# First norm of a hybrid encoder: mean squares for two token tiles at a time, and a later copy of the first weight tile's high half

## The chip, the cores and the metric

The kernel runs on one core of a Trainium2 chip. The metric is the device time of one execution in microseconds; lower is better. A core has five engines that work side by side, each through its own queue of instructions in order: TensorE (PE, with weight loads as PEld), VectorE (DVE), ScalarE (ACT), GpSimd (POOL) and SyncE (SP), which here issues the transfers. They wait for each other by semaphores.

## The reference

One encoder layer on 1024 + 512 tokens of width 1024, in float32. The change is in the first norm and the start of the projection that follows it:

```
u = x * rsqrt(mean(x * x) + 1e-6) * norm1
p = u @ W_in            # W_in: 1024 x 7696, for three mixers and their gates
x = x + W_out(sum_b sigmoid(G_b(u)) * (o_b @ W_br[b]))
x = x + relu(RMSNorm(x) @ W1)^2 @ W2
y = RMSNorm(x)
```

The three mixers are neighbourhood attention, a gated delta rule and a gated linear recurrence.

## The kernel before

Every large product is made of three float32r matmuls (`mm3`, L102 to L104): both factors are split into a high half, which is a rounded copy, and a low half, which is the rest. ScalarE makes the high halves, GpSimd the low ones.

The function `front` holds the first norm and the projection. The 1536 tokens are 12 tiles of 128. For each token tile j:

- ScalarE squares the tile and sums each row (`square`, L518), into column j of `ss`.
- VectorE makes mean + epsilon and its reciprocal for a group of G = 4 tiles at once (`mean`, L672 and L674), ScalarE the square root into `rstd` (L540).
- VectorE scales the tile by `rstd` into `xn`, which has two buffers (L695).
- TensorE transposes it in two halves of four 128 x 128 blocks into `turn` (`turn_half`, L612), in PSUM.
- VectorE multiplies by the norm's gain into `uf` (`gain_tile`, L686, two halves); this reads PSUM.
- ScalarE copies the high half into `u_hi` (L545), GpSimd subtracts to get `u_lo` (L488).

The weights come in column tiles of 128 (`load_w`), with `high_w` on ScalarE (L512) and `low_w` on GpSimd (L482), two buffers. TensorE first transposes tiles 0 to 3. Then it projects weight tiles 0 and 1 on three token blocks of 512 tokens, each behind `ul_done` of its four token tiles; within the first two blocks, one `turn_half` of the tiles 4 to 11 is put behind every second k step, that is behind every six matmuls. After that, weight tiles 2 to 60 are projected on all tokens. SyncE loads weight tile 2 only after `zeroed`, which GpSimd gives behind its last `u_lo`.

The queues are written out by hand. ScalarE's order at the start is: squares 0 to 3, high half of weight tile 0, then for each group its root, and for each tile in it the square of the tile four further on and the copy to `u_hi`; the high half of weight tile 1 follows tile 3. GpSimd's order is: low half of weight tile 0, `u_lo` of tiles 0 to 3, low half of weight tile 1, `u_lo` of tiles 4 to 11. VectorE's order within a group is `xn` of tile j, then the gain of tile j - 1; at the first tile of a group it is the gain of tile j - 1, the mean, then `xn` of tile j:

```
for j in range(NT):
    if j and j % G == 0:
        gain_tile(j - 1)
    if j % G == 0:
        mean(j)
    ...
    dve.tensor_scalar(xn[:, j % 2], x[:, j % XR], rstd[:, j:j + 1], None, ALU.mult).then_inc(normed, 1)
    if j % G:
        gain_tile(j - 1)
```

Of the kernel before, what the change touches and what calls it, by code (L numbers as in the profile page):

```python
# [17 lines left out]
ACT = mybir.ActivationFunctionType  # L18
ALU = mybir.AluOpType
# [3 lines left out]
D = 1024  # L23
# [3 lines left out]
NT = T // P  # L27
TB = 512
NTB = T // TB
EPS = 1e-6  # L30
# [206 lines left out]
def front(nc, sources, gain, w, proj, o_t, conv_w, conv_b, w_r, b_r, w_i, b_i, lam, u_hi, u_lo, ident, ones, rpb, v_mid, near,  # L237
# [6 lines left out]

    CT = BW // P
    G = 4
    XR = 8
    tiles = []
    for i in range(CT):
# [24 lines left out]
    with Space(nc, "pj") as s:  # L274
# [3 lines left out]
        with ExitStack() as early:  # L278
            def sb(name, shape):
                return early.enter_context(nc.sbuf_tensor(f"pj_{name}", [P] + shape, F32))  # L280
            x, xn, uf, junk = sb("x", [XR, D]), sb("xn", [2, D]), sb("uf", [2, KD, P]), sb("junk", [D])
        xpad, xc, gt = s.sb("xpad", [PADW]), s.sb("xc", [T]), s.sb("gt", [T])
# [14 lines left out]
        ss, ms, rr, rstd = (s.sb(v, [NT]) for v in ("ss", "ms", "rr", "rstd"))  # L297
# [43 lines left out]
        def _(sp):  # L341
            def load_x(t):
                if t >= XR:
                    sp.wait_ge(normed, t - XR + 1)
                sp.dma_start(x[:, t % XR], sources[t]).then_inc(x_in[t], 16)

            def load_w(n):
                if n >= 2:
                    sp.wait_ge(lo_done, n - 1)
                c = column(tiles[n])  # L350
                sp.dma_start(w_raw[:, n % 2], w_t[:, :, c:c + P]).then_inc(w_in[n % 2], 16)
# [49 lines left out]
            def bias_tables(p):  # L401
# [18 lines left out]
                if 26 <= p < 26 + NR:  # L420
# [5 lines left out]
                                 near[:, :, o * NA_COLS:o * NA_COLS + KEYS]).then_inc(bias_set, 16)  # L426
            for t in range(G):
                load_x(t)
                if t == 1:
                    sp.dma_start(gcol[:], gain.rearrange("(k p) -> p k", p=P), allow_slow_non_contiguous=True).then_inc(gained, 16)  # L430
            load_w(0)
            for t in range(G, NT):
                load_x(t)
                if t == G + 1:
                    load_w(1)
# [43 lines left out]
        def _(pool):  # L479
            def low_w(n):  # L480
                pool.wait_ge(hi_done, n + 1)
                pool.tensor_tensor(w_lo[:, n % 2], w_raw[:, n % 2], w_hi[:, n % 2].bitcast(F32), ALU.subtract).then_inc(lo_done, 1)  # L482
# [3 lines left out]
            for j in range(NT):  # L486
                pool.wait_ge(uh_done, j + 1)
                pool.tensor_tensor(u_lo[:, :, j * P:(j + 1) * P], uf[:, j % 2],  # L488
                                   u_hi[:, :, j * P:(j + 1) * P].bitcast(F32), ALU.subtract).then_inc(ul_done, 1)
                if j == G - 1:  # L490
                    low_w(1)
# [15 lines left out]
        def _(act):  # L507
            def high_w(n):
                act.wait_ge(w_in[n % 2], n // 2 * 16 + 16)
                if n >= 2:  # L510
                    act.wait_ge(mm_done, n - 1)
                act.copy(w_hi[:, n % 2], w_raw[:, n % 2]).then_inc(hi_done, 1)  # L512

            def square(j):
                act.wait_ge(x_in[j], 16)
                if j:
                    act.wait_ge(squared, j)
                act.activation(junk[:], x[:, j % XR], ACT.Square, accum_out=ss[:, j:j + 1]).then_inc(squared, 1)  # L518

# [6 lines left out]
            def decay(i, d):  # L526
# [5 lines left out]
                act.activation(rt[:], a[:], ACT.Square).then_inc(a2_done, 1)  # L532
                act.wait_ge(v_done, 2 * i + d + 1)
                act.activation(rt[:], rt[:], ACT.Sqrt).then_inc(rt_done, 1)
            for j in range(G):
                square(j)
            high_w(0)
            for j0 in range(0, NT, G):
                act.wait_ge(recip, j0 // G + 1)
                act.activation(rstd[:, j0:j0 + G], rr[:, j0:j0 + G], ACT.Sqrt).then_inc(rooted, 1)  # L540
                for j in range(j0, j0 + G):
                    if j + G < NT:
                        square(j + G)
                    act.wait_ge(scaled, 2 * j + 2)
                    act.copy(u_hi[:, :, j * P:(j + 1) * P], uf[:, j % 2]).then_inc(uh_done, 1)  # L545
                    if j == G - 1:
                        high_w(1)
# [120 lines left out]
        @block.vector  # L668
        def _(dve):
            def mean(j0):  # L670
                dve.wait_ge(squared, j0 + G)
                dve.tensor_scalar(ms[:, j0:j0 + G], ss[:, j0:j0 + G], 1.0 / D, EPS, ALU.mult, ALU.add).then_inc(rstd_in, 1)  # L672
                dve.wait_ge(rstd_in, j0 // G + 1)
                dve.reciprocal(rr[:, j0:j0 + G], ms[:, j0:j0 + G]).then_inc(recip, 1)  # L674
                dve.wait_ge(rooted, j0 // G + 1)

            def gain_tile(j):
                if j == 0:
                    dve.wait_ge(gained, 16)
                if j >= 2:  # L680
                    dve.wait_ge(uh_done, j - 1)
                    dve.wait_ge(ul_done, j - 1)
                for half in range(2):
                    k = slice(half * (KD // 2), (half + 1) * (KD // 2))
                    dve.wait_ge(turned, 2 * j + half + 1)
                    dve.tensor_tensor(uf[:, j % 2, k], turn[:, half], gcol[:, k].unsqueeze(2).to_broadcast([P, KD // 2, P]),  # L686
                                      ALU.mult).then_inc(scaled, 1)
            for j in range(NT):
                if j and j % G == 0:
                    gain_tile(j - 1)  # L690
                if j % G == 0:
                    mean(j)
                if j >= 2:
                    dve.wait_ge(turned, 2 * (j - 1))
                dve.tensor_scalar(xn[:, j % 2], x[:, j % XR], rstd[:, j:j + 1], None, ALU.mult).then_inc(normed, 1)  # L695
                if j % G:
                    gain_tile(j - 1)
            gain_tile(NT - 1)

# [400 lines left out]
def deltanet(nc, proj, g_rows, cols, masks, o_t, conv_w, norm_w, ident, ones):  # L1100
# [10 lines left out]
    with Space(nc, "dn") as s:  # L1111
# [151 lines left out]
        def _(act):  # L1263
# [29 lines left out]
            def main(i, more):  # L1293
# [23 lines left out]
                for k in range(NS):  # L1317
                    act.wait_ge(S["s_mm"], i * NS + k + 1)
                    if k == 0:
                        act.wait_ge(S["amat"], i * 12 + 12)  # L1320
                    if k >= 4:
                        act.wait_ge(S["u_mm"], i * VT + 6 + k - 3)
                    act.copy(sbuf_s[k % 4], ps[:, k % 2]).then_inc(S["s_ev"], 1)
                    if T_LAG <= k < NTR + T_LAG:
                        turned(k - T_LAG)
                    u = k + 2 * NTB
                    if i and u == OUT_AT["squares"]:
                        out_squares(i - 1)
                    if i and u == OUT_AT["root"]:
                        out_root(i - 1)  # L1330
                    if more:
                        front(i + 1, u)
                    if u == ZTANH_AT:
                        act.wait_ge(S["z_in"], i * 16 + 16)
                        act.activation(th[:, 1], zt, ACT.Tanh, scale=0.5).then_inc(S["zt"], 1)
# [14 lines left out]
            for u in range(UNITS):  # L1350
                front(0, u)
# [5 lines left out]
        def _(pe):  # L1357
# [29 lines left out]
            def main(i, more):  # L1387
# [40 lines left out]
                for step in range(NS + T_LAG):  # L1428
# [12 lines left out]
                    if U_LAG <= step < NS + U_LAG:  # L1441
                        k = step - U_LAG
                        n = k % 6
                        pe.wait_ge(S["s_ev"], i * NS + k + 1)

                        pe.wait_ge(S["u_ev"], i * VT + 6 + k - 1)
                        for j in range(4):
                            last = pe.matmul(ps[:, 5 + 2 * (k % 2), j], sbuf_s[k % 4][:, j], un[:, n, j], start=True, stop=True)
                        last.then_inc(S["u_mm"], 1)
                        if i and 6 + k == OUT_AT["lengths"]:  # L1450
                            out_lengths(i - 1)
                        if i and 6 + k in OUT_AT["spread"]:
                            out_spread(i - 1, OUT_AT["spread"].index(6 + k), 3)
                        if more:
                            front(i + 1, 6 + k)
# [883 lines left out]
```

## Time and profile before

| | |
|---|---|
| median of 3 runs | 3469.65 us (3467.18 to 3469.73) |
| the profiled execution | 3468.34 us, span 3466.6 us |
| TensorE matmuls busy | 3187.0 us, 92% of the span |
| VectorE, ScalarE, GpSimd busy | 1314.3, 1073.4, 1180.3 us |
| mean granted TensorE clock | 0.951 |

In the rows below, a row of the timeline gives the start in us from the span's start, the duration in us, the engine, the line and operation, what is written <- what is read, and how many instructions are merged (x). A bracket gives the idle time of the engine ahead of it and what ended that. A merged row's duration runs from the first start to the last end. A tile is named without its buffer, so the token tiles are told by their order.

### The profile page before, as it was taken

Reading aid. Unit: us, or ns where it says so; the run is one execution under the profiler, and the core shown is the slowest. Engines: PE = TensorE matmul, PEld = TensorE weight load, DVE = VectorE, ACT = ScalarE, POOL = GpSimd, SP = SyncE. Lnnn points to the kernel's source line nnn. Section 1 sums busy time; section 2 is a strip of 40 time slices with the busy share of each in tenths; the row PEclk is TensorE's granted clock in tenths of the full one; section 3 lists DMA queues with packets and bytes.
Section 4 is the critical chain, followed back from the end, with each engine's and each line's share of the span. In section 5 each row is a group of like instructions: output and inputs, shape, how many; then the busy total and the mean of one; then the engine's idle time right before and its main releaser. Section 6 shows DMA issues by size and latency. Waiting matters only on the chain. (4 is left out here: it accounts for less than half of the span.)

```text
span 3466.6 us, 40721 instructions
## 1 busy us (share of the span) xinstructions
PE 3187.0 (92%) x16275; PEld 2654.2 (77%) x16275; DVE 1314.3 (38%) x1975; ACT 1073.4 (31%) x1691; POOL 1180.3 (34%) x761
## 2 busy tenths in 40 slices
PE   6999999999998957969696979998999999999998
PEld 4888888888886636869595958786888888888887
DVE  4232323111001877575766433511222323232323
ACT  3222222321112734434343421223233333323222
POOL 4111111111113021121212014244666566666664
PEclk9999999999999977979797989998999999999999
DMA  3433233433323620001000045443332232333331
GB/s 110 164 131 107 77 110 99 128 100 118 130 79 143 201 95 28 19 28 37 28 19 1 19 143 170 140 143 118 98 98 97 85 98 97 122 98 97 97 122 61
DMA packets 235946, 334.04 MB, mean 96 GB/s; under 512 B 32368, under 2 KB 185712, under 8 KB 235760
## 3 DMA queue, kind: packets, MB, share of 16 engines
q1 hardware_dynamic: 235760, 331.44, 29.2%
q8 instruction: 131, 2.15, 0.2%
q14 instruction: 55, 0.45, 0.0%
HBM read 254.27 MB, written 86.93 MB: 98 GB/s over the span
## 5 line engine op out<-in xcount | busy, mean ns | idle before, releaser
L102 PE MATMUL pj_acc<-u_hi,pj_w_hi 128*128 128x512 f32 x1464 | 582.9, 398 | 14.7 <-POOL u_lo L488 13.0
L104 PE MATMUL pj_acc<-u_hi,pj_w_lo 128*128 128x512 f32 x1464 | 571.8, 391 | 0.0
L103 PE MATMUL pj_acc<-u_lo,pj_w_hi 128*128 128x512 f32 x1464 | 571.4, 390 | 0.0
L2256 DVE TENSOR_TENSOR x_tm<-m_ps,x_tm 128x512 f32<-128x512 f32 x384 | 265.0, 691 | 745.0 <-PE m_ps L104 745.0
L482 POOL TENSOR_TENSOR pj_w_lo<-pj_w_raw,pj_w_hi 128x1024 fp32r<-128x1024 f32 x61 | 148.0, 2427 | 826.3 <-ACT pj_w_hi L512 826.3
L102 PEld LDWEIGHTS pj_acc<-u_hi,pj_w_hi 128*128 128x128 f32 x1464 | 275.9, 188 | 77.8 <-POOL u_lo L488 13.9
L2133 POOL TENSOR_TENSOR m_w_lo<-m_w_raw,m_w_hi 128x1024 fp32r<-128x1024 f32 x96 | 237.6, 2498 | 263.2 <-ACT m_w_hi L2047 263.2
L103 PEld LDWEIGHTS pj_acc<-u_lo,pj_w_hi 128*128 128x128 f32 x1464 | 276.0, 189 | 61.8 <-issue 5.7
L104 PEld LDWEIGHTS pj_acc<-u_hi,pj_w_lo 128*128 128x128 f32 x1464 | 275.7, 188 | 57.8
L102 PE MATMUL m_ps<-m_v_hi,m_w_hi 128*128 128x512 f32 x768 | 299.9, 390 | 2.4 <-DVE m_v_lo L2224 2.4
L103 PE MATMUL m_ps<-m_v_lo,m_w_hi 128*128 128x512 f32 x768 | 299.7, 390 | 0.0
L104 PE MATMUL m_ps<-m_v_hi,m_w_lo 128*128 128x512 f32 x768 | 299.7, 390 | 0.0
L102 PE MATMUL m_ps<-m_w_hi,m_h_hi 128*128 128x512 f32 x768 | 299.6, 390 | 0.0
L104 PE MATMUL m_ps<-m_w_hi,m_h_lo 128*128 128x512 f32 x768 | 298.9, 389 | 0.0
L103 PE MATMUL m_ps<-m_w_lo,m_h_hi 128*128 128x512 f32 x768 | 298.8, 389 | 0.0
L2126 POOL TENSOR_TENSOR m_w_lo<-m_w_raw,m_w_hi 128x1024 fp32r<-128x1024 f32 x96 | 227.9, 2396 | 23.0 <-ACT m_w_hi L2040 23.0
L1865 POOL TENSOR_TENSOR mo_w_lo<-mo_w_raw,mo_w_hi 128x512 fp32r<-128x512 f32 x72 | 94.1, 1307 | 357.0 <-ACT mo_w_hi L1832 357.0
L512 ACT CAST pj_w_hi<-pj_w_raw 128x1024 fp32r<-128x1024 f32 x61 | 63.9, 1047 | 404.5 <-PE pj_acc L104 392.2
L2047 ACT CAST m_w_hi<-m_w_raw 128x1024 fp32r<-128x1024 f32 x96 | 96.0, 1049 | 247.8 <-PE m_ps L104 247.8
L102 PEld LDWEIGHTS m_ps<-m_v_hi,m_w_hi 128*128 128x128 f32 x768 | 144.8, 189 | 33.0 <-DVE m_v_lo L2224 2.8
L2059 ACT CAST m_h_hi<-m_rel 128x512 fp32r<-128x512 f32 x96 | 59.7, 622 | 356.4 <-POOL m_rel L2139 356.4
L104 PEld LDWEIGHTS m_ps<-m_v_hi,m_w_lo 128*128 128x128 f32 x768 | 144.7, 188 | 30.2
(258 smaller groups left out, 5605.4 us busy)
## 6 DMA issues: line engine op xcount, KB each, us to landing
m_w_raw<-in_w_mlp_dram SPq DMA_DIRECT2D x48, 1024.0 KB, 5.4
m_w_raw<-in_w_mlp_dram SPq DMA_DIRECT2D x96, 512.0 KB, 3.3
proj<-pj_stage SPq DMA_DIRECT2D x61, 768.0 KB, 3.4
pj_w_raw<-in_w_in_dram SPq DMA_DIRECT2D x61, 512.0 KB, 4.7
mo_gate<-proj SPq DMA_DIRECT2D x24, 768.0 KB, 4.2
mo_w_raw<-in_w_out_dram SPq DMA_DIRECT2D x48, 256.0 KB, 2.8
rpb_bias<-pj_shut SPq DMA_DIRECT2D x48, 192.0 KB, 3.0
rpb_bias<-rpb_near SPq DMA_DIRECT2D x24, 384.0 KB
```

The lines of the kernel that those rows point to most:

```text
L102: pe.matmul(out, w_hi, x_hi, start=first, stop=False)
L103: pe.matmul(out, w_hi, x_lo, start=False, stop=False)
L104: return pe.matmul(out, w_lo, x_hi, start=False, stop=last)
L482: pool.tensor_tensor(w_lo[:, n % 2], w_raw[:, n % 2], w_hi[:, n % 2].bitcast(F32), ALU.subtract).then_inc(lo_done, 1)
L512: act.copy(w_hi[:, n % 2], w_raw[:, n % 2]).then_inc(hi_done, 1)
L1865: pool.tensor_tensor(w_lo[:, sl % 2], w_raw[:, sl % 3], w_hi[:, sl % 2].bitcast(F32), ALU.subtract).then_inc(w_lo_done, 1)
L2047: act.copy(w2_hi[:, (2 * gg + j) % 4], w2_raw[:, j]).then_inc(w2_hi_done, 1)
L2059: act.copy(h_hi[:, m % 4], rel[:, j]).then_inc(hh_done, 1)
L2126: pool.tensor_tensor(w1_lo[:, m % 4], w1_raw[:, :, j * P:(j + 1) * P], w1_hi[:, m % 4].bitcast(F32), ALU.subtract).then_inc(w1_lo_done, 1)
L2133: pool.tensor_tensor(w2_lo[:, m % 4], w2_raw[:, j], w2_hi[:, m % 4].bitcast(F32), ALU.subtract).then_inc(w2_lo_done, 1)
L2256: dve.tensor_tensor(xt, ps2[:, q % 4], xt, ALU.add).then_inc(added, 1)
```

## The change

A second group size GS = 2 takes the place of G in ScalarE's and VectorE's queues: the mean, the reciprocal and the root are made for two tiles at a time, six times in place of three; ScalarE squares two tiles ahead in place of four. `high_w(0)` is moved from behind the first four squares to behind square 3, which now comes after the copy of tile 0 and ahead of the copy of tile 1. `high_w(1)`, the orders of TensorE, GpSimd and SyncE, and all shapes of large tiles stay as they are.

```diff
     G = 4
+    GS = 2
 ...
-            for j in range(G):
+            for j in range(GS):
                 square(j)
-            high_w(0)
-            for j0 in range(0, NT, G):
-                act.wait_ge(recip, j0 // G + 1)
-                act.activation(rstd[:, j0:j0 + G], rr[:, j0:j0 + G], ACT.Sqrt).then_inc(rooted, 1)
-                for j in range(j0, j0 + G):
-                    if j + G < NT:
-                        square(j + G)
+            for j0 in range(0, NT, GS):
+                act.wait_ge(recip, j0 // GS + 1)
+                act.activation(rstd[:, j0:j0 + GS], rr[:, j0:j0 + GS], ACT.Sqrt).then_inc(rooted, 1)
+                for j in range(j0, j0 + GS):
+                    if j + GS < NT:
+                        square(j + GS)
+                    if j == 1:
+                        high_w(0)
                     act.wait_ge(scaled, 2 * j + 2)
                     act.copy(u_hi[:, :, j * P:(j + 1) * P], uf[:, j % 2]).then_inc(uh_done, 1)
 ...
             def mean(j0):
-                dve.wait_ge(squared, j0 + G)
-                dve.tensor_scalar(ms[:, j0:j0 + G], ss[:, j0:j0 + G], 1.0 / D, EPS, ALU.mult, ALU.add).then_inc(rstd_in, 1)
+                dve.wait_ge(squared, j0 + GS)
+                dve.tensor_scalar(ms[:, j0:j0 + GS], ss[:, j0:j0 + GS], 1.0 / D, EPS, ALU.mult, ALU.add).then_inc(rstd_in, 1)
 ...
             for j in range(NT):
-                if j and j % G == 0:
+                if j and j % GS == 0:
                     gain_tile(j - 1)
-                if j % G == 0:
+                if j % GS == 0:
                     mean(j)
 ...
-                if j % G:
+                if j % GS:
                     gain_tile(j - 1)
```

## Rows read from the trace of the kernel before

**Rows 1.** Windows: busy time and count of each engine, then clock and DMA.

```profile
88.00:1100.00 1012.00, 1004.78 (x4344) 814.84 (x4342) 222.40 (x166) 209.84 (x192) 168.09 (x70) 1.00 0.34 109
```

**Rows 2.** Waits of TensorE from 0 to 90 us: total, times, longest.

```profile
PE pj_acc L102 <- POOL u_lo L488: 13.0, 3, 4.5
```

**Rows 3.** Timeline of ScalarE, 8 to 21 us.

```profile
8.55 0.19 ACT L518 ACTIVATION_READ_ACCUMULATOR pj_junk<-pj_x 128x1 f32 x1
...
13.06 1.04 ACT L512 CAST pj_w_hi<-pj_w_raw 128x1024 fp32r<-128x1024 f32 x1 [0.60 <-DMA pj_w_raw<-in_w_in_dram]
14.12 1.28 ACT L540 ACT_TABLE_LOAD   x1
15.41 0.20 ACT L540 ACTIVATE pj_rstd<-pj_rr 128x4 f32<-128x4 f32 x1
...
19.87 1.05 ACT L545 CAST u_hi<-pj_uf 128x1024 fp32r<-128x1024 f32 x1 [3.21 <-DVE pj_uf L686]
20.82 1.06 ACT L518 ACTIVATE pj_junk<-pj_x 128x1024 f32<-128x1024 f32 x1
```

**Rows 4.** Timeline of ScalarE around a later table load.

```profile
167.75 1.28 ACT L534 ACT_TABLE_LOAD   x1
169.64 1.49 ACT L534 ACTIVATE pj_rt<-pj_rt 128x1536 f32<-128x1536 f32 x1 [0.60 <-DVE pj_rt L721]
```

**Rows 5.** Timeline of VectorE, 15 to 18 us.

```profile
15.65 1.43 DVE L695 TENSOR_SCALAR pj_xn<-pj_x,pj_rstd 128x1024 f32<-128x1024 f32 x1 [2.78 <-ACT pj_rstd L540]
...
17.01 0.74 DVE L695 TENSOR_SCALAR pj_xn<-pj_x,pj_rstd 128x1024 f32<-128x1024 f32 x1
```

**Rows 6.** Timeline of GpSimd, 14 to 34 us.

```profile
14.19 2.35 POOL L482 TENSOR_TENSOR pj_w_lo<-pj_w_raw,pj_w_hi 128x1024 fp32r<-128x1024 f32 x1 [10.24 <-ACT pj_w_hi L512]
20.99 10.03 POOL L488 TENSOR_TENSOR u_lo<-pj_uf,u_hi 128x1024 fp32r<-128x1024 f32 x4 [4.46 <-ACT u_hi L545]
30.97 2.82 POOL L482 TENSOR_TENSOR pj_w_lo<-pj_w_raw,pj_w_hi 128x1024 fp32r<-128x1024 f32 x1
```

**Rows 7.** Timeline of three engines, group border ahead of tile 8.

```profile
47.65 0.69 DVE L686 TENSOR_TENSOR pj_uf<-pj_turn,pj_gcol 128x512 f32<-128x512 f32 x1 [1.04 <-PE pj_turn L612]
48.26 0.16 DVE L672 TENSOR_SCALAR pj_ms<-pj_ss 128x4 f32<-128x4 f32 x1
48.38 1.04 ACT L545 CAST u_hi<-pj_uf 128x1024 fp32r<-128x1024 f32 x1 [1.55 <-DVE pj_uf L686]
...
49.33 0.20 ACT L540 ACTIVATE pj_rstd<-pj_rr 128x4 f32<-128x4 f32 x1
49.50 2.34 POOL L488 TENSOR_TENSOR u_lo<-pj_uf,u_hi 128x1024 fp32r<-128x1024 f32 x1 [1.26 <-ACT u_hi L545]
...
49.56 2.83 DVE L695 TENSOR_SCALAR pj_xn<-pj_x,pj_rstd 128x1024 f32<-128x1024 f32 x1 [0.93 <-ACT pj_rstd L540]
```

**Rows 8.** Timeline of VectorE: second half of tile 5's gain.

```profile
40.35 0.69 DVE L686 TENSOR_TENSOR pj_uf<-pj_turn,pj_gcol 128x512 f32<-128x512 f32 x1 [1.04 <-PE pj_turn L612]
```

**Rows 9.** Timeline of TensorE: restarts and transposes of the first two blocks.

```profile
31.08 0.80 PE L102 MATMUL pj_acc<-u_hi,pj_w_hi 128*128 128x512 f32 x1 [4.48 <-POOL u_lo L488]
...
36.07 0.60 PE L612 MATMUL pj_turn<-ident,pj_xn 128*128 128x128 f32 x4
...
41.54 0.60 PE L612 MATMUL pj_turn<-ident,pj_xn 128*128 128x128 f32 x4
...
51.89 0.79 PE L102 MATMUL pj_acc<-u_hi,pj_w_hi 128*128 128x512 f32 x1 [4.28 <-POOL u_lo L488]
...
56.73 0.60 PE L612 MATMUL pj_turn<-ident,pj_xn 128*128 128x128 f32 x4
```

**Rows 10.** Windows, the restart of the second block.

```profile
51.80:54.60 2.80, 2.71 (x6) 2.04 (x7) 1.25 (x2) 0.00 (x0) 0.04 (x1) 0.50 0.00 0
```

**Rows 11.** Timeline of TensorE: first matmuls after two shorter waits.

```profile
86.88 0.50 PE L102 MATMUL pj_acc<-u_hi,pj_w_hi 128*128 128x512 f32 x1 [1.68 <-POOL pj_w_lo L482]
...
2250.36 0.80 PE L102 MATMUL mo_ps<-mo_w_hi,mo_held 128*128 128x512 f32 x1 [2.77 <-POOL mo_w_lo L1865]
```

More of the change, by code:

```diff
@@ L670, in mean @@
             def mean(j0):
-                dve.wait_ge(squared, j0 + G)
-                dve.tensor_scalar(ms[:, j0:j0 + G], ss[:, j0:j0 + G], 1.0 / D, EPS, ALU.mult, ALU.add).then_inc(rstd_in, 1)
-                dve.wait_ge(rstd_in, j0 // G + 1)
-                dve.reciprocal(rr[:, j0:j0 + G], ms[:, j0:j0 + G]).then_inc(recip, 1)
-                dve.wait_ge(rooted, j0 // G + 1)
+                dve.wait_ge(squared, j0 + GS)
+                dve.tensor_scalar(ms[:, j0:j0 + GS], ss[:, j0:j0 + GS], 1.0 / D, EPS, ALU.mult, ALU.add).then_inc(rstd_in, 1)
+                dve.wait_ge(rstd_in, j0 // GS + 1)
+                dve.reciprocal(rr[:, j0:j0 + GS], ms[:, j0:j0 + GS]).then_inc(recip, 1)
+                dve.wait_ge(rooted, j0 // GS + 1)
             def gain_tile(j):
```

## The prediction

> **What bounds the kernel now.** I read the page's waits of TensorE first, then the opening 90 us instruction by instruction on each engine, since every edit lies in the first norm. After that opening the front stage is all TensorE: it is busy 1004.78 of the 1012 us from 88 to 1100 [rows 1], so nothing behind can swallow time lost or won in front. In the opening, TensorE waits 13.0 us in three places for GpSimd's `u_lo` [rows 2]: before the first, second and third token block of the projection. The three waits are alike: TensorE turns the last tile of the next block, then VectorE's gain, ScalarE's `u_hi`, GpSimd's `u_lo` follow one another and TensorE starts. So the opening is one chain: start of the first block, then eight steps of six matmuls and four transposes, the wait, eight more steps, the wait. Weights two and on are loaded behind `zeroed`, which GpSimd gives after its last `u_lo`; they move with the chain. The time changes by what `u_lo` of tile 11 moves by.
>
> **Removed at the start.** ScalarE's first root stands behind four squares, the weight's high half and a table load; it starts at 15.41 [rows 3]. After the change it stands behind two squares. The second square's sum ends at 8.55 + 0.19 = 8.74. The table load of 1.28 us is put ahead of a single wait: elsewhere it ran from 167.75 and the square root it serves came 0.60 us after it ended, waiting for VectorE [rows 4]. So the load runs at once, hides the mean (0.16 us [rows 7]) and a reciprocal of like size, and the root starts at 10.03: 5.4 us earlier. That is all that could ever be won.
>
> **What is left of it.** From root to `u_hi` of tile 0 was 4.46 us, of which 1.43 - 0.74 = 0.69 is VectorE's first `xn` lying in wait while GpSimd's low half of the weight ran until 16.54 [rows 5, 6]. GpSimd is idle at 10 us, so `u_hi` starts at 10.03 + 3.77 = 13.80. But the weight's high half now stands behind the copy of tile 0 and square 3: 0.95 us for the copy (the next instruction starts at 20.82 behind 19.87) and 1.06 for the square with the short read of its sum partly under it put it at 15.83, and it ends at 16.87. GpSimd's queue has the low half in front of every `u_lo`: it runs from 16.96 to 19.31 (2.35 [rows 6]), and `u_lo` of tile 0 can start at 19.31 against 20.99. So only 1.7 of the 5.4 us are left: the copy was moved past, and took GpSimd's queue with it. The four `u_lo` took 10.03 us in a row. In them one instruction was stretched by a waiting `xn`; now a second `xn` (tile 2, whose root comes after the moved copy) waits for the low half and gets in ahead of the next one. Such a stretch costs 2.82 against 2.35, 0.47 us [rows 6]. The first block starts 1.7 - 0.5 = 1.2 us earlier. Bounds: 1.7 without the stretch, 0 if ScalarE's order delays tile 1 more than I see.
>
> **Added at tile 6 and tile 10.** With four in a group, `xn` of the next tile is issued ahead of the gain of the one before, except at tile 4 (in front of the first block, where it is hidden by GpSimd) and tile 8. At tile 8 the trace shows the price of a border [rows 7]: gain second half at 47.65, mean at 48.26, root at 49.33 because it stands behind the copy of tile 7 at 48.38, and `xn` at 49.56, where GpSimd's `u_lo` had started at 49.50. `xn` took 2.83 in place of 0.74: it came free only after the 2.34 us of `u_lo`. That is 49.56 + 2.83 - 47.65 = 4.74 us from gain to `xn`. At tile 8 it costs nothing: TensorE is waiting for the block anyway, and the next transposes come six matmuls later.
>
> Groups of two put the same border at tiles 6 and 10, in the midst of the eight steps, where TensorE's queue has the transposes between matmuls. Gain of tile 5 starts at 40.35 [rows 8]; plus 4.74 is 45.09, and the transposes of tile 6, which ran at 41.54 [rows 9], start at about 45.15: TensorE stands for 3.6 us. All matmuls of the first block stand behind them in order, then tile 7's transposes, and so `u_lo` of tile 7, which the second block waits for. None of it is hidden. Tile 10 repeats the pattern with the same steps in the second block: 3.6 again. The three small instructions of an extra border are in these 4.74 us; the squares that its mean needs stand in ScalarE's queue ahead of the copy of tile 5 and are ready. The extra border at tile 2 lies in front of the first block: its root waits for the copy of tile 1, and its `xn` then waits for the low half, which is the term of the start's sum above.
>
> What makes `xn` wait is weighed here against the skill. The row shows an `xn` of 2.83 us under a running `u_lo`, 0.74 otherwise, while the gain, which reads PSUM, keeps its 0.69 at all times. The Trainium skill, SBUF — State Buffer, section "Who interferes with whom", says that a two-port VectorE instruction and a GpSimd instruction take one port pair by lock for the whole instruction, whoever issues first. By that rule the trace agrees: `u_lo` led by 0.06 us at tile 8. By a lost lead the sum would be that of the second rival.
>
> **The clock.** At the blocks' starts TensorE comes back from 4.28 and 4.48 us of idleness at a granted clock of 0.50, 1.2 GHz [rows 10]. Restart to the second group of transposes took 56.73 - 51.89 = 4.84 and 36.07 - 31.08 = 4.99 us [rows 9]. At full clock three steps took 41.54 - 36.07 = 5.47, 1.82 each; the same stretch is two steps less one group of transposes (0.60 or under), 3.04 to 3.64. So a slow restart costs 1.2 to 1.9 us; I take 1.6. Does a stall of 3.6 us make the clock fall? After 2.77 us idle the first matmul took 0.80, as at half clock; after 1.68 it took 0.50 [rows 11]. 3.6 lies above the gap that was followed by a fall, so I take the fall at both: 3.2 us. The Trainium skill, TensorE: Matmul & The Clock Gate, section "What's actually happening", says that the slow state is the default, that activity releases it, and that the watch on activity does not start anew with a kernel. The trace agrees in that a gap of 2.77 us was enough; by this rule the two stalls could fare differently, which is the case of one escape below.
>
> **Sum.** -1.2 + 2 x 3.6 + 2 x 1.6 = +9.2 us. The profiled execution lasted 3468.34 (span 3466.6), so 3477.5; against the median of the runs, 3469.65, which is 1.3 above it, 3478.9. The rest of the kernel is unchanged.
>
> **Rivals.**
> - *The clock holds* through both stalls: +6.0, 3475.7. For it: the time of a fall follows something I can't place, and a gap of 1.68 left the clock alone. Against: the 2.77 us gap. If one stall of two escapes: +7.6, 3477.3.
> - *`xn` takes the port first.* At the border `xn` and `u_lo` are 0.06 us apart [rows 7]. If `xn` comes first it takes 0.74, gain to `xn` is 2.65, and each stall is 40.35 + 2.65 + 0.06 - 41.54 = 1.5 us, under the gap that left the clock alone. Sum -1.2 + 3.0 = +1.8, 3471.5: no change that can be told. Against: the same copy releases `u_lo` directly and `xn` only by way of a root of 0.20 us, so the order is built in.
> - *The early start wins* (the other side). If the borders at tiles 6 and 10 were ready in time, as the `xn` of four in a group are, only the gain of the start would be left, up to the whole 5.4 us if the low half also kept out of GpSimd's way. The point from which it decides: the transposes of tile 6 would have to be ready before 41.54, so the border below 1.2 us in place of 4.74. Its price in full is -5.4, 3464.3, under 0.2% too; with the low half in the way -1.2, 3468.5. Against: the low half's place in GpSimd's queue and the 4.74 us of a border [rows 6, 7].
> - *Slow restarts are dearer*: the fall comes late in a stall, the slow stretch lasts past a second group of transposes and the block's own restart changes too; 3 us each in place of 1.6, +12, 3481.7.
>
> **How the numbers follow.** A measurement of this kernel tells about 0.2%, 6.9 us, from no change; so 3476.6 is the border. Forecast (two stalls, both or one with a slow restart) 0.62; clock holds 0.14; port taken first 0.08; no stall on the chain or start wins 0.07; dearer 0.09. The slower cases are the forecast but for a tenth, the dear one, and a third of the held clock, +6.0 being so near the border: 0.56 + 0.09 + 0.04 = 0.69. The same: 0.28; faster needs 6.9 us of a possible 5.4: 0.03, for what I can't see. The range is 3473.0 to 3482.5: it leaves out the port rival below, and the worst restarts above.
>
> **What the profile would show.** Root of tiles 0 and 1 at about 10.0; the high half at 15.8; GpSimd's low half until 19.3; first `pj_acc` matmul at 29.9 (it was 31.08). `xn` of tile 6 and of tile 10 with 2.8 us, started just behind `u_lo`; transposes of tiles 6 and 10 with 3.6 us of idleness on TensorE released by `xn` L695; the second block's first matmul at about 51.9 - 1.2 + 3.6 + 1.6 = 55.9, the third's at 81.8; the wait ahead of each block still about 4.3. Wrong it would be if `xn` of tile 6 took 0.74, if the gap in front of its transposes were under 2 us, or if the third block started before 79.

## The result, and the profile after

The change makes the kernel slower: 3477.96 us median of 10 runs (3477.15 to 3479.68), against 3469.62 of 10 runs of the kernel before. The ratio is 1.0025 (95% interval 1.0015 to 1.0035), 8.3 us between the medians. The forecast was 3478.9, with a range of 3473.0 to 3482.5. The profiled execution has a span of 3476.3 us, 9.7 more than the one of before.

The waits of TensorE from 0 to 90 us (total, times, longest), after the change:

```profile
PE pj_turn L614 <- DVE pj_xn L697: 23.0, 4, 10.9
PE pj_acc L102 <- POOL u_lo L489: 13.0, 3, 4.5
```

Before, there was a single wait for `xn`, the one at the start:

```profile
PE pj_turn L612 <- DVE pj_xn L695: 17.1, 1, 17.1
```

The row for `u_lo` is as it was [rows 2]; the waits for `xn` are now four: the start, tile 2, and the two stalls in the blocks. ScalarE's and GpSimd's timelines of the start:

```profile
8.40 0.19 ACT L519 ACTIVATION_READ_ACCUMULATOR pj_junk<-pj_x 128x1 f32 x1
8.60 1.28 ACT L540 ACT_TABLE_LOAD   x1
9.89 0.20 ACT L540 ACTIVATE pj_rstd<-pj_rr 128x2 f32<-128x2 f32 x1
...
13.67 1.05 ACT L547 CAST u_hi<-pj_uf 128x1024 fp32r<-128x1024 f32 x1 [2.26 <-DVE pj_uf L688]
...
15.67 1.03 ACT L513 CAST pj_w_hi<-pj_w_raw 128x1024 fp32r<-128x1024 f32 x1
```

```profile
16.78 2.35 POOL L483 TENSOR_TENSOR pj_w_lo<-pj_w_raw,pj_w_hi 128x1024 fp32r<-128x1024 f32 x1 [12.85 <-ACT pj_w_hi L513]
19.09 10.45 POOL L489 TENSOR_TENSOR u_lo<-pj_uf,u_hi 128x1024 fp32r<-128x1024 f32 x4
```

The root comes 5.5 us earlier [rows 3], `u_lo` of tile 0 only 1.9 [rows 6], and the four `u_lo` take 10.45 in place of 10.03. The border at tile 6, all engines:

```profile
39.51 0.69 DVE L688 TENSOR_TENSOR pj_uf<-pj_turn,pj_gcol 128x512 f32<-128x512 f32 x1 [1.04 <-PE pj_turn L614]
...
40.23 1.05 ACT L547 CAST u_hi<-pj_uf 128x1024 fp32r<-128x1024 f32 x1 [1.56 <-DVE pj_uf L688]
...
41.19 0.20 ACT L540 ACTIVATE pj_rstd<-pj_rr 128x2 f32<-128x2 f32 x1
...
41.36 2.34 POOL L489 TENSOR_TENSOR u_lo<-pj_uf,u_hi 128x1024 fp32r<-128x1024 f32 x1 [1.27 <-ACT u_hi L547]
41.42 2.83 DVE L697 TENSOR_SCALAR pj_xn<-pj_x,pj_rstd 128x1024 f32<-128x1024 f32 x1 [0.94 <-ACT pj_rstd L540]
```

That is the pattern of tile 8 in [rows 7], to 0.01 us: `u_lo` leads by 0.06, `xn` takes 2.83. TensorE's timeline, the rows with a wait:

```profile
29.59 0.79 PE L102 MATMUL pj_acc<-u_hi,pj_w_hi 128*128 128x512 f32 x1 [4.47 <-POOL u_lo L489]
44.30 0.68 PE L614 MATMUL pj_turn<-ident,pj_xn 128*128 128x128 f32 x4 [3.44 <-DVE pj_xn L697]
56.30 0.79 PE L102 MATMUL pj_acc<-u_hi,pj_w_hi 128*128 128x512 f32 x1 [4.28 <-POOL u_lo L489]
71.26 0.66 PE L614 MATMUL pj_turn<-ident,pj_xn 128*128 128x128 f32 x4 [3.43 <-DVE pj_xn L697]
83.27 0.79 PE L102 MATMUL pj_acc<-u_hi,pj_w_hi 128*128 128x512 f32 x1 [4.28 <-POOL u_lo L489]
...
97.77 0.50 PE L102 MATMUL pj_acc<-u_hi,pj_w_hi 128*128 128x512 f32 x1 [0.58 <-POOL pj_w_lo L483]
...
2261.30 0.50 PE L102 MATMUL mo_ps<-mo_w_hi,mo_held 128*128 128x512 f32 x1 [2.77 <-POOL mo_w_lo L1867]
```

Against before the first block starts 1.5 us early (29.59, 31.08), the second 4.4 late (56.30, 51.89), the third 10.7 late (83.27, 72.60), weight tile 2 is 10.9 late (97.77, 86.88), and so are the later stages until 2261.30 (2250.36, +10.9). There 1.4 us come back: the wait of 2.77 us is the same in both, but before, the first matmul behind it took 0.80 us [rows 11] and now 0.50, and ten matmuls further on the distance between the two profiles is 9.5 us. At the end of the span it is 9.7.

### The profile page after: what moved, and what is told of

Read it like the earlier page. It is cut to its first block and busy times, and to the rows that moved or that the text cites. A ratio compares the mean times of both kernels' runs of the same rounds, so it can differ in the third digit from the quotient of the medians.

```text
span 3476.3 us, 40733 instructions
## 1 busy us (share of the span) xinstructions
PE 3192.5 (92%) x16275; PEld 2657.2 (76%) x16275; DVE 1320.7 (38%) x1981; ACT 1072.5 (31%) x1694; POOL 1179.9 (34%) x761
## 5 line engine op out<-in xcount | busy, mean ns | idle before, releaser
L102 PEld LDWEIGHTS pj_acc<-u_hi,pj_w_hi 128*128 128x128 f32 x1464 | 277.2, 189 | 77.1 <-POOL u_lo L489 13.9
L103 PEld LDWEIGHTS m_ps<-m_v_lo,m_w_hi 128*128 128x128 f32 x768 | 144.8, 189 | 30.2
```

The lines of the kernel that those rows point to most:

```text
L102: pe.matmul(out, w_hi, x_hi, start=first, stop=False)
L103: pe.matmul(out, w_hi, x_lo, start=False, stop=False)
```

## The experiments

Each was compared with the kernel before on the same chip. The changed kernel's own ratio (1.0025) is from another comparison, so what a run is worth against the changed kernel is reckoned by way of the kernel before. The diffs are cuts, against the changed kernel; two_start_early is built on two_start, early_wait on two_start_early, early_wait_fill on early_wait, and their diffs are against those. A "border" is the place where one group ends and the next one's mean and root are made. "Blocks" are the starts of TensorE's three token blocks in the profile; before: 31.08, 51.89, 72.60. `GR` is the list of group sizes that takes the place of `GS`; the loops then run over its groups, and as many squares are made ahead as the next group needs.

One thing has to be known to read the blocks. In the profiles, a block without a stall and without extra matmuls takes from 20.61 us (two_start_early, second) to 21.98 (early_wait, first), and the kernel before has 20.81 and 20.71. What differs is how long the slow clock lasts behind the block's start: six matmuls in both blocks of the kernel before, eleven in the first of move_only. The time from a block's first matmul to VectorE's second gain behind it (5.62 and 5.47 us before) measures this slow restart. So a difference of about 1 us in the length of one block is not put down to an edit here.

| run | blocks | median, us | before, us | ratio (95%) |
|---|---|---|---|---|
| group_only | 34.76, 60.94, 87.67 | 3482.90 | 3468.96 | 1.0042 (1.0030 to 1.0055) |
| move_only | 32.41, 54.21, 74.95 | 3471.33 | 3468.96 | 1.0003 (0.9994 to 1.0012) |
| one_border | 31.25, 58.07, 79.86 | 3473.49 | 3468.96 | 1.0014 (1.0005 to 1.0022) |
| filled | 30.28, 55.04, 79.37 | 3472.14 | 3468.96 | 1.0010 (1.0001 to 1.0018) |
| xn_first | 29.54, 52.86, 76.43 | 3470.15 | 3470.36 | 1.0006 (0.9997 to 1.0014) |
| root_first | 29.53, 52.59, 75.36 | 3470.83 | 3470.36 | 1.0002 (0.9993 to 1.0010) |
| two_start | 30.64, 51.91, 72.69 | 3467.22 | 3470.36 | 0.9991 (0.9982 to 1.0000) |
| two_start_early | 30.22, 50.93, 71.54 | 3468.52 | 3470.36 | 0.9996 (0.9987 to 1.0005) |
| all_borders | 31.13, 66.63, 104.06 | 3497.48 | 3468.71 | 1.0081 (1.0067 to 1.0094) |
| early_wait | 29.07, 51.05, 72.37 | 3466.39 | 3468.71 | 0.9996 (0.9987 to 1.0005) |
| early_wait_fill | 29.14, 50.12, 69.35 | 3465.28 | 3468.71 | 0.9988 (0.9979 to 0.9997) |

**group_only: the groups without the move.**

```diff
 for j in range(GS):
     square(j)
+high_w(0)
 ...
-        if j == 1:
-            high_w(0)
```

> Groups of two throughout, but the first weight tile's high half stays where it was, behind the first squares and ahead of the first root. The root of tiles 0 and 1 then waits for the weight's transfer as before, about 15.4 us; the copy of tile 0 comes at 19.9 and the root of tiles 2 and 3 behind the copy of tile 1, about 22.9, so that their xn meet GpSimd's u_lo. My theory: first block at 33.9 (31.08 before, +2.8), and two stalls with a slow restart at tiles 6 and 10, 5.3 to 6.3 us each: +13.4 to +15.4 us, about 3484. Rival (the groups bring the early start, the moved copy does nothing): first block at 29.6 as in the changed kernel, 3478.

The first block starts 3.7 us later than before (2.8 forecast), and the two blocks with an extra border are 5.4 and 6.0 us longer. Between the medians there are 13.9 us, as forecast. The groups alone do not bring an early start: in ScalarE's timeline the first root stands at 15.36 us, behind the weight's transfer as before, and the root of tiles 2 and 3 only at 23.54, behind the copy of tile 1.

**move_only: the move without the groups.**

```diff
-GS = 2
+GS = 4
```

> Groups of four as before, only the first weight tile's high half is moved behind the copy of tile 0 and the next square. My theory: the root of tiles 0 to 3 at about 13.8, copy of tile 0 at 17.5, high half at 19.5, GpSimd's low half until 23.0, so u_lo of tile 0 starts 2.0 us later than before; no stall at tiles 6 and 10. First block +1.5 to +2.0, time +1.5 to +2.0 us, about 3471.3. Rival (the earlier root wins): first block before 31.0, time at or under that of before.

The first block starts 1.3 us later than before, and no wait for `xn` stands in the blocks. The medians are 2.4 us apart; the interval reaches to no change. So either part alone costs time at the start (3.7 and 1.3 us), and both together win 1.5.

**one_border: one extra border.**

```diff
-GS = 2
+GR = (4, 2, 2, 4)   # and high_w(0) as in group_only
```

> Groups of 4, 2, 2 and 4 tiles, high half of the first weight tile where it was: the start of before, and one extra border, at tile 6. My theory: TensorE stalls 3.5 us there and restarts at half clock for 1.75 us; the rest as before: +5.2 us, up to +6.2 if the next block's restart is slow for longer, about 3475. Rival (the stall falls into the wait for the second block): 0. Rival (the clock holds): +3.5.

There is one stall, of 3.45 us, at tile 6. The first block is longer by 6.0 us (26.82 against 20.81); the second, which has no stall, by 1.1; the third block starts 7.3 us late. Between the medians there are 4.5 us (the interval is 1.7 to 7.6; 5.2 to 6.2 were forecast). So the stall falls into no wait. That it costs more than its idle time is seen in the profile; the interval of the times would also allow 3.5 us alone.

**filled: TensorE kept busy in the stalls.** The extra matmuls write nothing that is used.

```diff
         if k % 2 and turns:
+            if turns[0] in ((6, 0), (10, 0)):
+                for x in range(13):
+                    pe.matmul(acc[:, 2], w_hi[:, 0, x % KD], u_hi[:, x % KD, 0:TB], start=True, stop=True)
             turn_half(*turns.pop(0))
```

> The changed kernel with 13 more matmuls of 128x512 on TensorE ahead of the transposes of tile 6 and of tile 10, written to a bank that is cleared later; they lie in the 3.4 us that TensorE stands idle there and take about 3.0. Nothing else is changed. If the clock's fall is a cost of its own: both transposes at the time they had, but full clock behind them, 1.75 us less each: 3.5 us under the changed kernel, about 3474.5. If the stalls cost only their idle time: no change from the changed kernel, 3478. If the matmuls are too long for the gap: up to 1 us over.

The transposes of tile 6 came no earlier (44.62 us, 44.30 in the changed kernel), but the kernel is 3.2 us over the kernel before in place of 8.3. That makes it 5.1 us faster than the changed one by way of the kernel before; the two intervals (1.0001 to 1.0018, 1.0015 to 1.0035) still touch, so the profile is the surer witness. The same stretch behind the stall, in the windows of the changed kernel and then of this one (busy times and counts of PE, PEld, DVE, ACT, POOL, then the granted clock):

```profile
44.70:48.30 3.60, 3.60 (x14) 2.91 (x13) 0.91 (x2) 0.00 (x0) 0.00 (x0) 0.53 0.02 5
```

```profile
44.70:48.30 3.60, 3.60 (x20) 3.02 (x21) 1.92 (x3) 0.44 (x1) 0.00 (x0) 1.00 0.00 0
```

In the same time TensorE does 14 instructions at about half clock (0.53; 0.50 is 1.2 GHz) and 20 at full clock (2.4 GHz). From the transposes of tile 6 to the gain of tile 7 it is 4.44 us in place of 6.03, and from those of tile 10 to the gain of tile 11 it is 4.43 in place of 6.04: 3.2 us saved behind the two stalls, for 3.5 forecast. The blocks take 24.76 and 24.33 us in place of 26.71 and 26.97, 4.6 us less. The other 1.4 come from the blocks' own restarts, which lie ahead of the extra matmuls. The idle time left of each stall is 0.55 us.

**xn_first: VectorE ahead of GpSimd by a wait.**

```diff
     pool.wait_ge(uh_done, j + 1)
+    if j in (5, 9):
+        pool.wait_ge(normed, j + 2)
```

> The changed kernel with one wait more: GpSimd holds u_lo of tile 5 until xn of tile 6 is written, and u_lo of tile 9 until that of tile 10. So VectorE always comes first at the two borders. Port theory: xn takes 0.74 in place of 2.83 us, the transposes of tiles 6 and 10 are late by 1.5 us each in place of 3.4, the clock holds as after the gap of 1.68: first block 29.6, then -1.5 + 2 x 1.5 = +1.5 us on the kernel before, about 3471. Rival (the border's order of mean, root and xn is the cost, whoever has the port): stalls of 3.4 us stay, 3478.

```profile
42.44 0.66 PE L620 MATMUL pj_turn<-ident,pj_xn 128*128 128x128 f32 x4 [1.36 <-DVE pj_xn L707]
52.86 0.79 PE L102 MATMUL pj_acc<-u_hi,pj_w_hi 128*128 128x512 f32 x1 [4.28 <-POOL u_lo L491]
66.02 0.66 PE L620 MATMUL pj_turn<-ident,pj_xn 128*128 128x128 f32 x4 [1.36 <-DVE pj_xn L707]
```

In TensorE's timeline the stalls are 1.36 us, and the next transposes follow 1.89 us behind those of tile 6, at full-clock pace (3.04 in the changed kernel). `u_lo` waits in place of `xn`, and with the borders still there most of the slowdown is gone: the ratio is 1.0006 in place of 1.0025, its interval lies under that of the changed kernel, and the medians are level. (In the profile the third block is 3.8 us late: the stalls add 2.7, the start takes 1.5 off, and the rest are slow restarts of the blocks, 6.53 and 6.79 us to the second gain.) So which of `xn` and `u_lo` goes first decides, not the order of mean, root and `xn`.

**root_first: VectorE ahead of GpSimd by ScalarE's order.** The root at the head of these groups is left out in return.

```diff
     for j in range(j0, j0 + gs):
         ...
+        if nxt and j == j0 + gs - 1 and j > 3:
+            act.wait_ge(recip, q + 2)
+            act.activation(rstd[:, j + 1:j + 1 + nxt], rr[:, j + 1:j + 1 + nxt], ACT.Sqrt).then_inc(rooted, 1)
         act.wait_ge(scaled, 2 * j + 2)
         act.copy(u_hi[:, :, j * P:(j + 1) * P], uf[:, j % 2]).then_inc(uh_done, 1)
```

> The changed kernel with ScalarE's root of the next group put ahead of the copy of the last tile of the group, from tile 5 on (tiles 5, 7 and 9). Theory: the root runs right behind the reciprocal, 0.5 us behind gain of tile 5, xn starts 0.6 us ahead of u_lo and takes the port: stall of 0.65 us at tiles 6 and 10. The copies of tiles 5, 7 and 9 come 0.4 us later, which the second and third block pay: -1.5 + 2 x (0.65 + 0.4) = +0.6 us, about 3470. Rival (xn is slow for another cause than GpSimd's lead): stalls stay above 2.5 us, 3476 or more.

The stalls are 0.69 and 0.68 us, and the wait for the second block is 4.94 us in place of 4.28. As forecast, the time can't be told from that of the kernel before. So a second way of letting `xn` go first takes most of the stalls away too.

**two_start: groups of two for the start alone.**

```diff
-GS = 2
+GR = (2, 2, 4, 4)
```

> Groups of 2, 2, 4 and 4 tiles, high half of the first weight tile where the change puts it: the changed start, without the borders at tiles 6 and 10. Theory: first block at 29.6 as in the changed kernel, no stall in the blocks: -1.5 us on the kernel before, about 3467.7. Rival (the start's gain is lost before the third block in any case): 3469 to 3470.

There is no stall, and the median is 3.1 us under the kernel before, at the edge of the interval. The profile does not bear these 3.1 us out: the first block starts 0.44 us early and restarts slowly, so the second and third start at 51.91 and 72.69 us where they did before (51.89, 72.60). In the profile that is the rival's case, though the median is the one of the theory. And the first block came at 30.64, not at 29.6. ScalarE's timeline shows why: the group of four behind needs two squares ahead of each copy, and the second one is over only at 27.14 us, where tile 3's gain is ready at 26.26.

```profile
26.08 1.06 ACT L519 ACTIVATE pj_junk<-pj_x 128x1024 f32<-128x1024 f32 x1
27.04 0.19 ACT L519 ACTIVATION_READ_ACCUMULATOR pj_junk<-pj_x 128x1 f32 x1
27.14 1.03 ACT L551 CAST u_hi<-pj_uf 128x1024 fp32r<-128x1024 f32 x1
```

**two_start_early: the low half out of `u_lo`'s way.**

```diff
-        if j == 1:
+        if j == 0:
             high_w(0)
```

> As two_start, but the first weight tile's high half stands behind square 2, ahead of the copy of tile 0: it waits for its transfer and runs from 13.0, GpSimd's low half is done at 16.5, u_lo of tile 0 starts 2.6 us earlier than in the changed kernel. Theory of the low half in GpSimd's way alone: first block at 27.0, -4.1 us, about 3465. Theory that xn of tile 3 is then what is late: it waits behind u_lo of tile 1 until about 22.2 (22.4 in the changed kernel), so copy and u_lo of tiles 2 and 3 hardly move: first block at 29.4, about 3467.5.

GpSimd's timeline: `u_lo` of tile 0 starts 2.5 us earlier than in the changed kernel, and then GpSimd stands idle for `u_hi` of tile 2.

```profile
16.57 5.12 POOL L489 TENSOR_TENSOR u_lo<-pj_uf,u_hi 128x1024 fp32r<-128x1024 f32 x2
24.60 2.35 POOL L489 TENSOR_TENSOR u_lo<-pj_uf,u_hi 128x1024 fp32r<-128x1024 f32 x1 [2.90 <-ACT u_hi L551]
```

In VectorE's queue the gain of tile 2 stands behind `xn` of tile 3, which ends only at 22.24 us. The first block moves by 0.4 us (30.64 to 30.22) against two_start; 27.0 and 29.4 were the two forecasts. So the second theory is much the nearer: the early low half uncovers the next wait, `xn` of tile 3 behind `u_lo` of tile 1. Past 29.4 it is the same two squares of ScalarE as in two_start: GpSimd waits another 0.87 us for `u_hi` of tile 3. The time can't be told from that of before.

**all_borders: the cost many times over.**

```diff
+GR = (4, 1, 1, 1, 1, 1, 1, 1, 1)   # and high_w(0) as in group_only
```

> The suspected cost many times over: the first group has four tiles, each tile after it is a group of its own; the high half of the first weight tile stays where it was. The start is that of before; borders at tiles 5, 6, 7 and 9, 10, 11 stand between matmuls (those at 4 and 8 lie in waits for a block). Theory: six stalls of 3.4 us, each with a restart at half clock of 1.75: +31 us, about 3501. If the clock holds: +21, 3491. If only the first stall of a block counts, as the rest would fall into it: +10.

The median is 28.8 us over the kernel before. The row of TensorE's waits for `xn` holds the start's 17.2 us and six stalls, 19.2 us in sum (three of 3.44 us, the others shorter):

```profile
PE pj_turn L617 <- DVE pj_xn L704: 36.4, 7, 17.2
```

The third block is 31.5 us late, 12.3 more than the idle time. Behind each of the six stalls matmuls of 0.63 us follow, where 0.39 is the full-clock time; this and the blocks' own restarts make 2 us for each stall. So each border costs again; 31 us were forecast, with six stalls of 3.4.

**early_wait: `xn` of tile 3 ahead.**

```diff
     pool.wait_ge(uh_done, j + 1)
+    if j == 1:
+        pool.wait_ge(normed, 4)
```

> two_start_early with one wait more: GpSimd holds u_lo of tile 1 until xn of tile 3 is written. Theory that xn of tile 3 behind u_lo of tile 1 is what was late there: xn of tiles 2 and 3 run one behind the other at 19 to 20, u_lo of tile 1 starts at 20.1 and the rest follow without a gap: first block at 27.5 to 28.1, 3 us under the kernel before, about 3466. Rival (GpSimd's order can't be bettered by waiting, it has 2.35 us for each of five instructions in any case): 30.2 as in two_start_early, 3468.

```profile
16.64 2.35 POOL L491 TENSOR_TENSOR u_lo<-pj_uf,u_hi 128x1024 fp32r<-128x1024 f32 x1
20.35 2.35 POOL L491 TENSOR_TENSOR u_lo<-pj_uf,u_hi 128x1024 fp32r<-128x1024 f32 x1 [1.36 <-DVE pj_xn L707]
23.45 2.35 POOL L491 TENSOR_TENSOR u_lo<-pj_uf,u_hi 128x1024 fp32r<-128x1024 f32 x1 [0.75 <-ACT u_hi L553]
26.67 2.35 POOL L491 TENSOR_TENSOR u_lo<-pj_uf,u_hi 128x1024 fp32r<-128x1024 f32 x1 [0.87 <-ACT u_hi L553]
```

GpSimd waits 1.36 us for `xn` and is the earlier for it: the first block starts at 29.07, 1.15 us better than in two_start_early, and 1.0 to 1.6 us short of the forecast, since the copies now leave gaps of 0.75 and 0.87. The time can't be told from that of before, and in the profile the 2.0 us won at the first block are down to 0.2 at weight tile 2 (86.69 against 86.88): the two blocks take 21.98 and 21.32 us, with a longer stretch of slow clock behind each start.

**early_wait_fill: the clock held over the waits for the blocks too.** The extra matmuls write nothing that is used.

```diff
+    if tb:
+        for x in range(16):
+            pe.matmul(acc[:, 2], w_hi[:, 0, x % KD], u_hi[:, x % KD, 0:TB], start=True, stop=True)
     pe.wait_ge(ul_done, G * (tb + 1))
```

> early_wait, and 16 more matmuls of 128x512 on TensorE in each of the waits for the second and the third block (4.28 us idle; the matmuls take 3.7 and write a bank that is cleared later). Theory of the clock as a cost of its own: the second and third block start at full clock and save 1.6 us each: 3.2 us under early_wait, about 3463. Rival (the restart's slowness is not the clock's): no change from early_wait.

```profile
50.12 0.50 PE L102 MATMUL pj_acc<-u_hi,pj_w_hi 128*128 128x512 f32 x1 [0.66 <-POOL u_lo L492]
...
69.35 0.50 PE L102 MATMUL pj_acc<-u_hi,pj_w_hi 128*128 128x512 f32 x1 [0.66 <-POOL u_lo L492]
82.82 0.50 PE L102 MATMUL pj_acc<-u_hi,pj_w_hi 128*128 128x512 f32 x1 [2.26 <-POOL pj_w_lo L484]
```

Both blocks start at full clock and keep it: the second gain of the second block comes 3.97 us behind its first matmul, against 6.09 in early_wait. Weight tile 2 begins 3.9 us before that of early_wait (86.69). Of these, 1.0 is the first block (20.98 against 21.98 us), ahead of any extra matmul, which leaves 2.9 for the extra matmuls. But the wait ahead of weight tile 2 grew from 1.55 to 2.26 us, and behind it the clock fell after all:

```profile
85.00:86.00 1.00, 1.00 (x4) 0.81 (x3) 0.00 (x0) 0.00 (x0) 0.11 (x1) 0.50 0.77 172
```

At the attention's first matmul 2.2 us of the 3.9 were left (1100.39 against 1102.56), and the medians are 1.1 us apart where 3.2 were forecast, less than the scatter of either (8 to 10 us). It is the one version whose whole interval lies under the kernel before, by 0.12% (0.03% to 0.21%).

## Why the prediction was right

- **The chain.** Right. The time followed the last `u_lo`, and the stage behind it took nothing up: the distance from weight tile 2 to attention is 1015.9 us in both profiles.
- **Removed at the start, and what is left.** Right in each step: root 9.89 (10.03 forecast), copy of tile 0 at 13.67 (13.80), high half 15.67 (15.83), low half done 19.13 (19.31), one `u_lo` more stretched (+0.42 for +0.47). The first block was 1.5 us early, not 1.2; 0.15 of it is the first transfers' landing, earlier in this execution (second square's sum read at 8.40, 8.55 before). move_only and group_only show that the parts need each other.
- **The stalls.** 3.44 and 3.43 us, forecast 3.6. one_border shows that a stall is not absorbed; xn_first and root_first show that its length hangs on whether `u_lo` or `xn` goes first. The rival of the port taken first was worked out as +1.8 us; forced, it gave 3470.15 us, with stalls of 1.36 where 1.5 was said. It did not come about by itself: `u_lo` led by 0.06 us again.
- **The clock.** Right that it falls at both stalls, but the reason given is weaker than it was put: a gap of 2.77 us, which the prediction took as enough on the word of one profile, was followed by a fall at that place in 5 of 13 profiles. Stalls of 2.77 us and more among these blocks, 11 in four profiles (changed kernel, group_only, one_border, all_borders), were all followed by one; waits of 1.91 us and less in the same stretch, by none, and one of 2.26 us (early_wait_fill) by one. In size the term was too small: it was 2 x 1.6 = 3.2 us in the sum and measured 2.5 + 2.8 = 5.3, what the blocks grew by (5.90 and 6.26) beyond the stalls. Some 1.65 us of each lie behind the stall, as I took it: from the transposes of tile 6 to the gain of tile 7 6.03 us against 4.38, and for tiles 10 and 11 6.04 against 4.40. The rest is the restart of the block itself, which held the slow clock for longer than before: from the first matmul to the second gain of the block 6.25 us against 5.62, and 6.53 against 5.47. The kernels without an extra border show that this varies by itself: in move_only the first block needs 6.60 us to its second gain, in early_wait 6.77. So the profile of before happened to have quick restarts, and the comparison of one profile with one charges the change for it.
- **The sum.** -1.5 + 5.9 + 6.3 + 0.2 = +10.9 at weight tile 2 in the profile, of which 1.4 are given back at 2261 us. +9.2 was forecast, 9.7 is the difference of the spans and 8.3 that of the medians (5.2 to 12.1 by the interval). That the number is so near is in part luck: the block restarts were dearer by 1.7 us, and a later fall of the clock stayed away.
- **The other side.** The early start exists at the first block and is small: 0.4, 0.9 and 2.0 us in two_start, two_start_early and early_wait, which have it without the stalls. At weight tile 2 their profiles have 0.1, 1.7 and 0.2 us of it. The medians are 3.1, 1.8 and 2.3 us under the kernel before, and none of the three is clear of no change; that a gain of the start alone reaches the end of the kernel is not shown. What keeps it small was named in part only (the low half in GpSimd's queue); two_start_early and early_wait show the next two limits, `xn` of tile 3 behind `u_lo`, then the squares ahead of ScalarE's copies.

## What to carry to other kernels

A smaller group brings its first result earlier and puts its border in more places; look at what the in-order queues have between the borders, and price each border from one that the trace already shows. Where two engines exclude each other on a resource, a lead of 0.06 us can cost 2 us: a wait that lets the short instruction on the critical path go first may be worth more than starting everything at once. A stall of TensorE can cost more than its length (those of 3.4 us did here, those of 1.36 us did not), and a saving of a few microseconds can be lost or doubled at a later wait.

## What the runs showed of the hardware

- After one and the same wait of 2.77 us, TensorE's first matmul took 0.80 us in the profiles of before, move_only, group_only, root_first and early_wait_fill, and 0.50 in those of the changed kernel, one_border, filled, xn_first, two_start, two_start_early, early_wait and all_borders. In the window 2200 to 2300 us the granted clock was 0.98 before and 1.00 in the changed kernel. So the length of the gap alone does not tell whether the clock falls; I had read [rows 11] as if it did. The fall can also come after the gap: behind the 4.28 us ahead of move_only's second block the first three matmuls took 0.50, 0.39 and 0.40 us, and from the fifth on they took 0.63.
- With GpSimd ahead by 0.06 us, `xn` took 2.83 us. xn_first shows the other side: with VectorE first, its two `xn` in a row took 1.42 us together, not stretched, and `u_lo` of tile 5, which started beside the second of them, took 2.76 us where that of tile 4 took 2.39. The Trainium skill, SBUF — State Buffer, section "Who interferes with whom", names issue order as what decides who blocks; both cases agree with it.
- Thirteen matmuls of no use in each of two stalls of TensorE held the clock at full speed behind them (granted 1.00 in place of 0.53) and brought the slowdown from 8.3 to 3.2 us (medians against the kernel before).
